# One GpSimd instruction of 1024 columns, with one signal, in place of two of 512 for the low part of a weight tile

## The chip, the cores and the metric

The kernel runs on one core of one Trainium2 chip. The metric is the device time of one execution in microseconds (us). The kernel before takes 1486.04 us, the median of three runs (1485.71 to 1487.81).

## The reference

The reference is one inference step of a two-layer decoder trunk with four parallel token mixers. There are 512 prompt tokens and 8 sample tokens, so every activation has 520 columns once it is transposed. What matters here, per layer:

```python
mod = silu(c) @ ada_w + ada_b                       # shift, scale, gate
h = rms_norm(x, norm_g) * (1.0 + scale) + shift
proj = einsum('btd,de->bte', h, w_in)               # (520, 1024) @ (1024, 7560)
oA, oB, oC, oD = rwkv7(...), retention(...), rglru(...), gated_delta(...)   # each 256 wide
up = einsum('btnw,nwd->btnd', stack(oA, oB, oC, oD), w_up)
merged = sum_n(sigmoid(gl) * up)                    # gl: the last 4 * 1024 columns of proj
x = x + gate * (merged @ w_out)
```

Two such layers are followed by an RMSNorm. All of it is in float32.

## The kernel before, in words

**Tiles and parts.** The products with `w_in`, `w_out` and `ada_w` are made in two parts: weights and activations are each split into a high part (a rounded copy) and a low part (the rest), and TensorE (PE) sums high by high, low by high and high by low. A weight tile is 1024 rows by 128 columns, in SBUF 128 partitions by 1024 columns. It comes by a transfer that SyncE issues (`load`, L559 for `ada_w`, L576 for `w_out` and `w_in`), then ScalarE (ACT) casts it to the high part (`split`, L1441), then GpSimd (POOL) subtracts the high part from it and leaves the low part in the place of the weights (L710). There are 94 tiles in layer 0 and 78 in layer 1: 30 `proj`, 32 `gate` and 8 `out` in each, and 24 or 8 `ada`, which make the next modulation rows. GpSimd does nothing else but clear some tiles at the start.

**Order of use on PE.** `product` (L838 and L846) takes a `proj`, `gate` or `out` tile in 12 parts: eight parts of four matmuls with the high part (k = 0 to 7), then four parts of four matmuls with the low part. It waits for GpSimd's first half ahead of low k = 0 and for the second half ahead of low k = 4. `ada` (L1373, L1376) has two matmuls with the high part and two with the low part, with a wait ahead of each of the latter. Tiles go through three ring slots, five in the last stage; a load into a slot is issued when PE has finished the tile that was there, and ACT splits a tile only when PE has finished with an earlier high part. Every engine works through its list in the order in which the code has it, and all signals are semaphores counted.

**The merge tail.** After the mixers a layer has 14 last lift products, `up(18)` to `up(31)` (L888), with an `ada` tile behind most of them (layer 1: behind the last eight), and then the eight `out` products. `up(n)` waits until VectorE (DVE) has emptied the PSUM pair that `up(n-2)` used. For each `up` DVE runs L1911 (reads PSUM and one SBUF tile) and L1912 (the same), and from `up(25)` on also `m_lo` (L1894): it subtracts the high part of a finished merged row from the row, both in SBUF. ACT makes that high part in `m_hi` (L1799), behind the split of the next weight tile in its list. The text numbers the eight `m_lo` from 0 to 7. `out(0)` is the first product that needs them, one for each k. In SyncE's list a `load` stands behind `bring_back` (L600), which waits for DVE's merged rows, and behind the end of the tile on PE whose slot it refills.

**Elsewhere.** In the trees (triangular solves) of the mixers DVE merges blocks with predicated copies (L797, L798), which PE waits for (L774), with parts of `proj` and `gate` tiles put between them. Ahead of the retention mixer DVE applies the rotation (L2277, L2279, L2281, L2289).

Of the kernel before, what the change touches and what calls it, by code (L numbers as in the profile page):

```python
# [19 lines left out]
KT = D_MODEL // P  # L20
# [57 lines left out]
def build_program(nc, a, o, order):  # L78
# [5 lines left out]
    mult, add, sub = ALU.mult, ALU.add, ALU.subtract  # L84
    ctx = ExitStack()
    tracks = {}
    with ctx:
# [193 lines left out]
        def ring_slot(kind, n, L):  # L281

            r = L.place[kind, n]
            return L.slot[r], (L.w[L.slot[r]], 16 * L.loads[r])

        def first_load(sp, n, L, layer):

            s, (arrived, _) = ring_slot("proj", n, L)
            col, _, _ = PROJ[n]
            sp.dma_start(RS[s], a["w_in"][layer, :, col:col + P].rearrange("(k p) c -> p k c", p=P)).then_inc(arrived, 16)  # L290
# [40 lines left out]
        @block.sync  # L331
        def _(sp):
            sp.dma_start(RC[0:8, 2:4, 0:512], a["c_sample"].rearrange("p (a c) -> p a c", a=2)).then_inc(s_c, 16)
            sp.dma_start(RC[8:9, 2:4, 0:512], a["c_prompt"].rearrange("p (a c) -> p a c", a=2)).then_inc(s_c, 16)
            sp.dma_start(cst[:, 0:384], a["consts"][:, 0:384]).then_inc(s_const, 16)
            sp.dma_start(RC[0:8, 0:2, 0:512], a["x_sample"][:, 0, :].rearrange("p (a c) -> p a c", a=2)).then_inc(s_c, 16)
            sp.dma_start(prow[0:PARAM_N, :], a["param_rows"][0]).then_inc(s_par, 16)
            lo = CONST_COLS["kdec"][0]
            sp.dma_start(cst[:, lo:CONST_N], a["consts"][:, lo:CONST_N]).then_inc(s_const, 16)
            for t in range(4):  # L340
                sp.dma_start(hT[:, 2 * t:2 * t + 2, 0:512], a["x_prompt"][0, t * P:(t + 1) * P, :].rearrange("p (a c) -> p a c", a=2)).then_inc(s_x, 16)
            for e in range(8):
                sp.dma_start(pairs[e], a["ada_w"][0, 512 * (e % 2):512 * (e % 2) + 512, 512 * (e // 2):512 * (e // 2) + 512]
                             .rearrange("(k p) c -> p k c", p=P)).then_inc(s_ada0[e], 16)
            for n in range(RING):
                first_load(sp, n, LAYERS[0], 0)
            sp.wait_ge(*dve0.at("x", KT - 1))
            for half in (slice(0, 4), slice(4, 8)):
                sp.dma_start(scrX[:, half, :], xT[:, half, :]).then_inc(LAYERS[0].xout, 16)
            sp.dma_start(cst[:, 384:lo], a["consts"][:, 384:lo]).then_inc(s_const2, 16)  # L350
            sp.dma_start(wv(10, 14 * P), a["tree_masks"]).then_inc(s_const2, 16)
# [112 lines left out]
        for layer, L in enumerate(LAYERS):  # L464
# [8 lines left out]
            aw, pw = TR["act_w"], TR["pool_w"]  # L473
            pm, am, dm = TR["pe_m"], TR["act_m"], TR["dve_m"]
            ps_, as_, ds = TR["pe_s"], TR["act_s"], TR["dve_s"]
            def ada_bank(b):

                return 2 if b in (1, 3) else 1
# [5 lines left out]
            def tile_part(ap, x):  # L484

                if x[0] == "proj" and PROJ[x[1]][1] == "ba":
                    return ap[:, :, 0:64].rearrange("p k (e c) -> p k e c", e=2)[:, :, :, 0:HEADS]
                return ap
# [215 lines left out]
            @block.gpsimd  # L704
            def _(pool):
                for q, (kind, n) in enumerate(SPLIT):
                    s, _ = ring_slot(kind, n, L)
                    pool.wait_ge(*aw.at("hi", q))
                    for k in (slice(0, KT // 2), slice(KT // 2, KT)):
                        nc.gpsimd.tensor_tensor(tile_part(RL[s][:, k], (kind, n)), tile_part(RS[s][:, k], (kind, n)), tile_part(HS[L.hslot[q]][:, k], (kind, n)), sub).then_inc(*pw.step("lo"))  # L710

# [104 lines left out]
            def _(pe):  # L818
# [5 lines left out]
                def product(out, x, kind, n, hi, lo, m=P, wait=None, parts=range(PARTS)):  # L824


                    s, _ = ring_slot(kind, n, L)
                    q = SPLACE[kind, n]
                    cols = lambda ap, h: ap[:, h * HALF:(h + 1) * HALF]
                    for p in parts:  # L830
                        if p == 0:
                            pe.wait_ge(*aw.at("hi", q))
                        if p < KT:
                            if wait:
                                pe.wait_ge(*wait(p))
                            for part in (hi, lo):
                                for h in x:
                                    nc.tensor.matmul(out(h), HS[L.hslot[q]][:, p, 0:m], cols(part(p), h), start=(p == 0 and part is hi), stop=False)  # L838
                            continue
                        if p == KT:  # L840
                            pe.wait_ge(*pw.at("lo", 2 * q))
                        elif p == KT + 2:
                            pe.wait_ge(*pw.at("lo", 2 * q + 1))
                        for k in (2 * (p - KT), 2 * (p - KT) + 1):
                            for h in x:
                                last = nc.tensor.matmul(out(h), RL[s][:, k, 0:m], cols(hi(k), h), start=False, stop=(k == KT - 1))  # L846
                    return last if parts[-1] == PARTS - 1 else None
# [516 lines left out]
                def ada(n):  # L1364

                    q, b, kp = SPLACE["ada", n], n // 4, n % 4
                    s, _ = ring_slot("ada", n, L)
                    out = psB[0:18, ada_bank(b), :]
                    pe.wait_ge(*aw.at("hi", q))
                    if b >= 2 and kp == 0:  # L1370
                        pe.wait_ge(*act_f.at("modrow", b - 1 if b == 5 else b - 2))
                    for k in range(2):
                        nc.tensor.matmul(out, chl[:, 2 * kp + k, :], wide(HS[L.hslot[q]])[:, k, :], start=(kp == 0 and k == 0), stop=False)  # L1373
                    for k in range(2):
                        pe.wait_ge(*pw.at("lo", 2 * q + k))
                        last = nc.tensor.matmul(out, chl[:, 2 * kp + k, :], wide(RL[s])[:, k, :], start=False, stop=(kp == 3 and k == 1))  # L1376
                    last.then_inc(*pe_f.step("ada"))
                    if kp == 1 and b:
                        mods(b - 1)
# [1048 lines left out]
    'pe_p0': 'proj proj proj proj proj proj proj proj proj proj proj proj proj proj proj proj proj proj proj proj proj proj proj proj proj proj proj proj proj proj'.split(),  # L2428
    'act_p0': 'proj proj proj proj proj proj proj proj proj proj proj proj proj proj proj proj proj proj proj proj proj proj proj proj proj proj proj proj proj proj'.split(),
    'act_w0': 'hi hi hi hi hi hi hi hi hi hi hi hi hi hi hi hi hi hi hi hi hi hi hi hi hi hi hi hi hi hi hi hi hi hi hi hi hi hi hi hi hi hi hi hi hi hi hi hi hi hi hi hi hi hi hi hi hi hi hi hi hi hi hi hi hi hi hi hi hi hi hi hi hi hi hi hi hi hi hi hi hi hi hi hi hi hi hi hi hi hi hi hi hi hi'.split(),  # L2430
    'pool_w0': 'lo lo lo lo lo lo lo lo lo lo lo lo lo lo lo lo lo lo lo lo lo lo lo lo lo lo lo lo lo lo lo lo lo lo lo lo lo lo lo lo lo lo lo lo lo lo lo lo lo lo lo lo lo lo lo lo lo lo lo lo lo lo lo lo lo lo lo lo lo lo lo lo lo lo lo lo lo lo lo lo lo lo lo lo lo lo lo lo lo lo lo lo lo lo lo lo lo lo lo lo lo lo lo lo lo lo lo lo lo lo lo lo lo lo lo lo lo lo lo lo lo lo lo lo lo lo lo lo lo lo lo lo lo lo lo lo lo lo lo lo lo lo lo lo lo lo lo lo lo lo lo lo lo lo lo lo lo lo lo lo lo lo lo lo lo lo lo lo lo lo lo lo lo lo lo lo lo lo lo lo lo lo lo lo lo lo lo lo'.split(),
    'pe_n0': 'mean var var var'.split(),
    'act_n0': 'sq ln rn tz sq ln rn tz tz sq ln rn tz'.split(),
    'dve_n0': 'cen normed gains bonus siluz gated normed siluz gated siluz gated normed siluz gated'.split(),
# [21 lines left out]
    'pe_p1': 'proj proj proj proj proj proj proj proj proj proj proj proj proj proj proj proj proj proj proj proj proj proj proj proj proj proj proj proj proj proj'.split(),  # L2456
    'act_p1': 'proj proj proj proj proj proj proj proj proj proj proj proj proj proj proj proj proj proj proj proj proj proj proj proj proj proj proj proj proj proj'.split(),
    'act_w1': 'hi hi hi hi hi hi hi hi hi hi hi hi hi hi hi hi hi hi hi hi hi hi hi hi hi hi hi hi hi hi hi hi hi hi hi hi hi hi hi hi hi hi hi hi hi hi hi hi hi hi hi hi hi hi hi hi hi hi hi hi hi hi hi hi hi hi hi hi hi hi hi hi hi hi hi hi hi hi'.split(),
    'pool_w1': 'lo lo lo lo lo lo lo lo lo lo lo lo lo lo lo lo lo lo lo lo lo lo lo lo lo lo lo lo lo lo lo lo lo lo lo lo lo lo lo lo lo lo lo lo lo lo lo lo lo lo lo lo lo lo lo lo lo lo lo lo lo lo lo lo lo lo lo lo lo lo lo lo lo lo lo lo lo lo lo lo lo lo lo lo lo lo lo lo lo lo lo lo lo lo lo lo lo lo lo lo lo lo lo lo lo lo lo lo lo lo lo lo lo lo lo lo lo lo lo lo lo lo lo lo lo lo lo lo lo lo lo lo lo lo lo lo lo lo lo lo lo lo lo lo lo lo lo lo lo lo lo lo lo lo lo lo'.split(),
    'pe_n1': 'mean var var var'.split(),  # L2460
    'act_n1': 'sq ln rn tz sq ln rn tz tz sq ln rn tz'.split(),
    'dve_n1': 'cen normed gains bonus siluz gated normed siluz gated siluz gated normed siluz gated'.split(),
# [108 lines left out]
```

## Time and profile before

| | |
|---|---|
| median of three runs | 1486.04 us |
| the profiled execution | 1487.9 us, of it 1486.1 us from the first to the last instruction |
| PE busy | 1406.4 us, 95% |
| DVE, ACT, POOL busy | 652.1, 517.0, 466.5 us |
| granted TensorE clock, mean | 0.981 of full speed |

Busy times say how much an engine did, not whether anything waited for it. The chain that ended last, and who waited for whom, say what set the time. In rows of a timeline the first number is the start in us from the first instruction, the second the time to the end of the last of the "xN" instructions that the row merges; in brackets stands the idle time before the first and what ended it.

### The profile page before, as it was taken

What the parts mean: (1) busy time and instruction counts of PE and PEld (TensorE: products, weight loads), DVE (VectorE), ACT (ScalarE), POOL (GpSimd) and SP (SyncE); (2) the same over time, 40 slices, a digit from 0 to 9 for tenths busy, and PEclk for the clock granted to TensorE, in tenths of its full rate; (3) what the DMA queues carried; (4) which work ended last, traced back from release to release, by engine and by line L of the source; (5) the groups of instructions that cost most, each with busy time, mean ns of one, the idle gap of its engine ahead of it and who ended that gap; (6) DMA issues with size and microseconds to landing.
All of it is one profiled execution on the core that took longest, in us unless ns stands there. A gap on an engine that the chain in (4) does not pass through costs nothing.

```text
span 1486.1 us, 33569 instructions
## 1 busy us (share of the span) xinstructions
PE 1406.4 (95%) x14880; PEld 1275.5 (86%) x14880; DVE 652.1 (44%) x1157; ACT 517.0 (35%) x780; POOL 466.5 (31%) x350
## 2 busy tenths in 40 slices
PE   6799999999999999998979999999999999998896
PEld 4699999989889998876879998999898998987695
DVE  5757423317234335746133951231444341655712
ACT  5534422225422245144443352222443123523312
POOL 0244422224212223147833452222322222312720
PEclk9899999999999999999999999999999999999998
DMA  9533231215321263376743323112263126346721
GB/s 318 196 86 97 68 91 45 59 45 118 102 81 45 68 128 98 117 221 215 228 143 86 98 74 84 45 45 73 65 153 85 45 59 103 99 143 176 222 86 58
DMA packets 275908, 162.18 MB, mean 109 GB/s; under 512 B 86102, under 2 KB 244922, under 8 KB 275252
## 3 DMA queue, kind: packets, MB, share of 16 engines
q1 hardware_dynamic: 274100, 159.06, 39.2%
q8 instruction: 117, 1.92, 0.5%
q10 hardware_dynamic: 1664, 0.98, 0.3%
q14 instruction: 27, 0.22, 0.0%
HBM read 135.25 MB, written 24.89 MB: 108 GB/s over the span
## 4 chain that ended last, share of the span: by engine, by line
PE 84%; DVE 6%; ACT 4%; DMA 2%; issue 2%; ACTq 1%; SPq 0%; POOL 0%; DVEq 0%
PE psA L838 35%; PE psA L846 18%; PE psA L888 6%; PE psB L774 3%; PE psB L784 3%; PE psB L783 3%; PE psB L719 2%; PE psB L962 1%; DMA RB<-in_ada_w 1%; PE psB L972 1%; PE psB L1376 1%; PE psB L1373 1%; PE psB L1404 1%; ACT w_hi L1441 1%; DMA RB<-in_w_out 1%
## 5 line engine op out<-in xcount | busy, mean ns | idle before, releaser
L710 POOL TENSOR_TENSOR w_lo<-ring,w_hi 128x512 fp32r<-128x512 f32 x274 | 372.4, 1381 | 901.9 <-ACT w_hi L1441 843.9
L838 PE MATMUL psA<-h_hi,w_hi 128*128 128x260 f32 x1984 | 427.4, 297 | 23.2 <-DVE h_lo L1856 13.1
L838 PE MATMUL psA<-h_lo,w_hi 128*128 128x260 f32 x1984 | 403.5, 285 | 0.0
L838 PEld LDWEIGHTS psA<-h_hi,w_hi 128*128 128x128 f32 x1984 | 309.2, 191 | 39.8 <-issue 19.6
L838 PEld LDWEIGHTS psA<-h_lo,w_hi 128*128 128x128 f32 x1984 | 310.1, 191 | 0.2
L846 PE MATMUL psA<-h_hi,w_lo 128*128 128x260 f32 x1984 | 274.5, 286 | 0.0
L846 PEld LDWEIGHTS psA<-h_hi,w_lo 128*128 128x128 f32 x1984 | 249.6, 187 | 5.3 <-issue 1.0
L1441 ACT CAST w_hi<-ring 128x1024 fp32r<-128x1024 f32 x133 | 137.2, 1033 | 14.1 <-PE psA L846 4.1
L789 ACT COPY ws<-psB 128x128 f32<-128x128 f32 x80 | 21.4, 268 | 243.9 <-PE psB L774 243.9
L797 DVE COPY_PREDICATED tg<-tmask,psB 128x128 f32<-128x128 uint8 x40 | 14.3, 357 | 127.2 <-PE psB L784 77.4
L1471 ACT ACTIVATE tg<-psA 128x520 f32<-128x520 f32 x48 | 28.9, 601 | 87.9 <-PE psA L846 87.7
L797 DVE COPY_PREDICATED ws<-tmask,psB 128x128 f32<-128x128 uint8 x40 | 14.3, 356 | 83.4 <-PE psB L784 46.8
L2354 DVE SCALAR_TENSOR_TENSOR xT<-psA,modT,xT 128x260 f32<-128x260 f32 x16 | 7.8, 488 | 90.1 <-PE psA L846 90.0
L710 POOL TENSOR_TENSOR w_lo<-ring,ra_lo 128x512 fp32r<-128x512 f32 x28 | 37.6, 1363 | 22.9 <-ACT ra_lo L1441 22.9
L710 POOL TENSOR_TENSOR rb_lo<-RB,ra_lo 128x512 fp32r<-128x512 f32 x20 | 25.5, 1300 | 42.1 <-ACT ra_lo L1441 42.1
L784 PE MATMUL psB<-tg,ws 64*64 64x32 f32 x640 | 37.4, 220 | 0.0
L784 PE MATMUL psB<-ws 64*64 64x32 f32 x640 | 37.4, 220 | 0.0
L888 PE MATMUL psA<-RB,upw 128*128 128x260 f32 x128 | 32.3, 396 | 3.6 <-DVE RA L1912 3.2
L1456 ACT COPY RA<-psA 128x520 f32<-128x520 f32 x18 | 10.7, 593 | 66.8 <-PE psA L846 61.6
L888 PEld LDWEIGHTS psA<-RB,upw 128*128 128x128 f32 x128 | 24.2, 194 | 10.4 <-DVE RA L1912 4.2
L784 PEld LDWEIGHTS psB<-tg,ws 64*64 64x64 f32 x640 | 32.1, 135 | 1.1
L784 PEld LDWEIGHTS psB<-ws 64*64 64x64 f32 x640 | 32.1, 135 | 1.1
(476 smaller groups left out, 2332.1 us busy)
## 6 DMA issues: line engine op xcount, KB each, us to landing
ring<-in_w_in SPq DMA_DIRECT2D x122, 512.0 KB, 4.2
scr_tanh<-tg SPq DMA_DIRECT2D x48, 260.0 KB, 4.5
ring<-in_ada_w SPq DMA_DIRECT2D x18, 512.0 KB, 5.2
upw<-in_w_up SPq DMA_DIRECT2D x64, 128.0 KB, 3.6
RA<-scr_tanh SPq DMA_DIRECT2D x30, 260.0 KB, 3.6
RB<-in_ada_w SPq DMA_DIRECT2D x14, 512.0 KB, 5.0
ws<-scr_tanh SPq DMA_DIRECT2D x24, 260.0 KB, 3.9
ring<-in_w_out SPq DMA_DIRECT2D x9, 512.0 KB, 4.9
```

The lines of the kernel that those rows point to most:

```text
L710: nc.gpsimd.tensor_tensor(tile_part(RL[s][:, k], (kind, n)), tile_part(RS[s][:, k], (kind, n)), tile_part(HS[L.hslot[q]][:, k], (kind, n)) ...
L719: last = nc.tensor.matmul(psB[:, k, 0:HALF], bones, s4[:, k, :], start=True, stop=True)
L774: last = nc.tensor.matmul(meet(psB[sd(g), 2, q * CH:(q + 1) * CH], lv, 0), At[sd(g), q, :], meet(T4[sd(g), q, :], lv, 0), start=True, stop ...
L783: nc.tensor.matmul(meet(psB[sd(g), 2, q * CH:(q + 1) * CH], lv, 0), V4[sd(g), q, :], meet(Y4[sd(g), q, :], lv, 0), start=True, stop=True)
L784: last = nc.tensor.matmul(meet(psB[sd(g), 2, 256 + q * CH:256 + (q + 1) * CH], lv, 1), Y4[sd(g), q, :], meet(V4[sd(g), q, :], lv, 1), star ...
L789: nc.scalar.copy(meet(q64(Y), lv, 0), meet(q64(psB[:, 2, 0:256]), lv, 0)).then_inc(*ta.step("y"))
L797: nc.vector.copy_predicated(meet(q64(T), lv, 0), bc(meet(tmask[:, lv, :], lv, 0), 1, 4), meet(q64(psB[:, 2, 0:256]), lv, 0))
L838: nc.tensor.matmul(out(h), HS[L.hslot[q]][:, p, 0:m], cols(part(p), h), start=(p == 0 and part is hi), stop=False)
L846: last = nc.tensor.matmul(out(h), RL[s][:, k, 0:m], cols(hi(k), h), start=False, stop=(k == KT - 1))
L888: last = nc.tensor.matmul(out(hf), upw[:, idx % UP_RING, i, :], outs[MERGE[idx][0]][:, i, hf * HALF:(hf + 1) * HALF], start=(i == 0), stop ...
L1441: nc.scalar.copy(tile_part(HS[L.hslot[q]], SPLIT[q]), tile_part(RS[s], SPLIT[q])).then_inc(*aw.step("hi"))
L1471: A(half(th_tile(idx)), psA[:, b:b + 2, 0:HALF], ACT.Tanh, scale=0.5).then_inc(*am.step("th"))
```

## The change

GpSimd makes the low part of a tile in one instruction over all eight k instead of two over four each, and signals once. PE waits for that one signal ahead of the first matmul with the low part, in `product` and in `ada`. The lists of signals are cut to half (`pool_w0` from 188 to 94 names, `pool_w1` from 156 to 78).

```diff
                     pool.wait_ge(*aw.at("hi", q))
-                    for k in (slice(0, KT // 2), slice(KT // 2, KT)):
-                        nc.gpsimd.tensor_tensor(tile_part(RL[s][:, k], (kind, n)), tile_part(RS[s][:, k], (kind, n)), tile_part(HS[L.hslot[q]][:, k], (kind, n)), sub).then_inc(*pw.step("lo"))
+                    nc.gpsimd.tensor_tensor(tile_part(RL[s], (kind, n)), tile_part(RS[s], (kind, n)), tile_part(HS[L.hslot[q]], (kind, n)), sub).then_inc(*pw.step("lo"))
...
                         if p == KT:
-                            pe.wait_ge(*pw.at("lo", 2 * q))
-                        elif p == KT + 2:
-                            pe.wait_ge(*pw.at("lo", 2 * q + 1))
+                            pe.wait_ge(*pw.at("lo", q))
...
+                    pe.wait_ge(*pw.at("lo", q))
                     for k in range(2):
-                        pe.wait_ge(*pw.at("lo", 2 * q + k))
                         last = nc.tensor.matmul(out, chl[:, 2 * kp + k, :], wide(RL[s])[:, k, :], start=False, stop=(kp == 3 and k == 1))
```

## Rows read from the trace of the kernel before

**Rows 1.** The page: busy time by engine, and the chain that ended last

```profile
PE 1406.4 (95%) x14880; PEld 1275.5 (86%) x14880; DVE 652.1 (44%) x1157; ACT 517.0 (35%) x780; POOL 466.5 (31%) x350
...
PE 84%; DVE 6%; ACT 4%; DMA 2%; issue 2%; ACTq 1%; SPq 0%; POOL 0%; DVEq 0%
```

**Rows 2.** PE's waits: waiting tile and line, releaser: total us, times, longest

```profile
PE psA L838 <- DVE merged_lo L1894: 4.9, 4, 1.5
...
PE psA L888 <- DVE RA L1912: 4.0, 4, 2.0
...
PE psB L1376 <- POOL rb_lo L710: 1.5, 2, 0.8
```

**Rows 3.** Line L710: count, duration ns min/median/max, first and last start

```profile
L710 POOL TENSOR_TENSOR w_lo<-ring,ra_lo x28: 1264/1286/1757, 662.6 to 1426.0; 128x512 fp32r<-128x512 f32 x28
```

**Rows 4.** GpSimd's groups by shape: count, busy us, mean ns of one, idle before

```profile
L710 POOL TENSOR_TENSOR w_lo<-ring,w_hi 128x32 fp32r<-128x32 f32 x4 | 0.9, 252 | 0.0
```

**Rows 5.** Line L846: all idle time of its engine before it, us and times

```profile
  issue: 1.0, 6
```

**Rows 6.** Timelines, layer 0, `out` stage: an `ada` tile on GpSimd and on PE

```profile
718.55 2.53 POOL L710 TENSOR_TENSOR rb_lo<-RB,ra_lo 128x512 fp32r<-128x512 f32 x2 [0.94 <-ACT ra_lo L1441]
...
721.95 0.62 PE L1376 MATMUL psB<-rb_lo,c_parts 128*18 128x512 f32 x2
```

**Rows 7.** Timelines, layer 0, the first `ada` tile on GpSimd and on PE

```profile
652.69 3.75 POOL L710 TENSOR_TENSOR rb_lo<-RB,ra_lo 128x512 fp32r<-128x512 f32 x3 [16.27 <-ACT ra_lo L1441]
...
655.26 0.40 PE L1376 MATMUL psB<-rb_lo,c_parts 128*18 128x512 f32 x1 [0.83 <-POOL rb_lo L710]
```

**Rows 8.** Line L1894 (all 16 `m_lo`): mean ns after the busy time

```profile
L1894 DVE TENSOR_TENSOR merged_lo<-mg,merged_hi 128x520 fp32r<-128x520 f32 x10 | 14.5, 1468 | 6.1 <-ACT merged_hi L1799 6.1
...
L1894 DVE TENSOR_TENSOR ra_lo<-RA,merged_hi 128x520 fp32r<-128x520 f32 x6 | 9.3, 1552 | 8.5 <-ACT merged_hi L1799 8.5
...
L2158 DVE TENSOR_TENSOR RD<-RD,ws 128x512 f32<-128x512 f32 x4 | 2.6, 684 | 0.0
```

**Rows 9.** DVE's timeline in the merge tail of layer 0

```profile
679.26 1.35 DVE L1894 TENSOR_TENSOR ra_lo<-RA,merged_hi 128x520 fp32r<-128x520 f32 x1 [4.47 <-ACT merged_hi L1799]
...
689.36 1.34 DVE L1894 TENSOR_TENSOR merged_lo<-mg,merged_hi 128x520 fp32r<-128x520 f32 x1 [1.55 <-ACT merged_hi L1799]
...
698.59 3.06 DVE L1894 TENSOR_TENSOR merged_lo<-mg,merged_hi 128x520 fp32r<-128x520 f32 x2 [0.23 <-ACT merged_hi L1799]
```

**Rows 10.** GpSimd's timeline in the same tail

```profile
678.78 2.96 POOL L710 TENSOR_TENSOR w_lo<-ring,ra_lo 128x512 fp32r<-128x512 f32 x2 [0.46 <-ACT ra_lo L1441]
...
688.87 2.98 POOL L710 TENSOR_TENSOR w_lo<-ring,ra_lo 128x512 fp32r<-128x512 f32 x2 [1.27 <-ACT ra_lo L1441]
...
698.13 2.96 POOL L710 TENSOR_TENSOR rb_lo<-RB,w_hi 128x512 fp32r<-128x512 f32 x2
```

**Rows 11.** PE's timeline in the same tail

```profile
682.02 2.02 PE L888 MATMUL psA<-RB,upw 128*128 128x260 f32 x8 [1.25 <-DVE RA L1912]
...
701.70 0.51 PE L838 MATMUL psA<-merged_hi,ra_lo 128*128 128x260 f32 x2 [0.94 <-DVE merged_lo L1894]
```

**Rows 12.** SyncE's timeline in the same tail: two issues of `w_out` tiles

```profile
683.10 0.40 SPq L576 DMA_DIRECT2D ring<-in_w_out  x1
...
691.75 0.37 SPq L576 DMA_DIRECT2D RB<-in_w_out  x1
```

**Rows 13.** Windows: length, busy PE, PEld, DVE, ACT, POOL, granted clock, DMA

```profile
675.00:692.00 17.00, 15.47 (x70) 10.30 (x70) 11.05 (x12) 8.52 (x12) 14.31 (x10) 1.00 0.90 291
1385.00:1400.00 15.00, 13.05 (x55) 8.55 (x53) 9.47 (x11) 6.77 (x9) 10.82 (x9) 0.89 0.81 254
1406.00:1423.00 17.00, 14.50 (x102) 13.84 (x103) 8.31 (x12) 3.93 (x6) 8.30 (x6) 0.90 0.33 104
```

**Rows 14.** Timelines of GpSimd, DVE and PE in the first tree of layer 0

```profile
190.73 2.57 POOL L710 TENSOR_TENSOR w_lo<-ring,w_hi 128x512 fp32r<-128x512 f32 x2 [9.99 <-ACT w_hi L1441]
...
191.08 1.23 DVE L798 COPY_PREDICATED tg<-tmask,ws 128x128 f32<-128x128 uint8 x1
...
193.16 0.54 PE L774 MATMUL psB<-tg,ws 64*64 64x32 f32 x12
```

**Rows 15.** DVE's timeline at the rotation in layer 0

```profile
572.52 2.33 DVE L2279 SCALAR_TENSOR_TENSOR RB<-RB,cst 128x520 f32<-128x520 f32 x2
```

More of the change, by code:

```diff
@@ L2430 @@
     'act_w0': 'hi hi hi hi hi hi hi hi hi hi hi hi hi hi hi hi hi hi hi hi hi hi hi hi hi hi hi hi hi hi hi hi hi hi hi hi hi hi hi hi hi hi hi hi hi hi hi hi hi hi hi hi hi hi hi hi hi hi hi hi hi hi hi hi hi hi hi hi hi hi hi hi hi hi hi hi hi hi hi hi hi hi hi hi hi hi hi hi hi hi hi hi hi hi'.split(),
-    'pool_w0': 'lo lo lo lo lo lo lo lo lo lo lo lo lo lo lo lo lo lo lo lo lo lo lo lo lo lo lo lo lo lo lo lo lo lo lo lo lo lo lo lo lo lo lo lo lo lo lo lo lo lo lo lo lo lo lo lo lo lo lo lo lo lo lo lo lo lo lo lo lo lo lo lo lo lo lo lo lo lo lo lo lo lo lo lo lo lo lo lo lo lo lo lo lo lo lo lo lo lo lo lo lo lo lo lo lo lo lo lo lo lo lo lo lo lo lo lo lo lo lo lo lo lo lo lo lo lo lo lo lo lo lo lo lo lo lo lo lo lo lo lo lo lo lo lo lo lo lo lo lo lo lo lo lo lo lo lo lo lo lo lo lo lo lo lo lo lo lo lo lo lo lo lo lo lo lo lo lo lo lo lo lo lo lo lo lo lo lo lo'.split(),
+    'pool_w0': 'lo lo lo lo lo lo lo lo lo lo lo lo lo lo lo lo lo lo lo lo lo lo lo lo lo lo lo lo lo lo lo lo lo lo lo lo lo lo lo lo lo lo lo lo lo lo lo lo lo lo lo lo lo lo lo lo lo lo lo lo lo lo lo lo lo lo lo lo lo lo lo lo lo lo lo lo lo lo lo lo lo lo lo lo lo lo lo lo lo lo lo lo lo lo'.split(),
     'pe_n0': 'mean var var var'.split(),
@@ L2458 @@
     'act_w1': 'hi hi hi hi hi hi hi hi hi hi hi hi hi hi hi hi hi hi hi hi hi hi hi hi hi hi hi hi hi hi hi hi hi hi hi hi hi hi hi hi hi hi hi hi hi hi hi hi hi hi hi hi hi hi hi hi hi hi hi hi hi hi hi hi hi hi hi hi hi hi hi hi hi hi hi hi hi hi'.split(),
-    'pool_w1': 'lo lo lo lo lo lo lo lo lo lo lo lo lo lo lo lo lo lo lo lo lo lo lo lo lo lo lo lo lo lo lo lo lo lo lo lo lo lo lo lo lo lo lo lo lo lo lo lo lo lo lo lo lo lo lo lo lo lo lo lo lo lo lo lo lo lo lo lo lo lo lo lo lo lo lo lo lo lo lo lo lo lo lo lo lo lo lo lo lo lo lo lo lo lo lo lo lo lo lo lo lo lo lo lo lo lo lo lo lo lo lo lo lo lo lo lo lo lo lo lo lo lo lo lo lo lo lo lo lo lo lo lo lo lo lo lo lo lo lo lo lo lo lo lo lo lo lo lo lo lo lo lo lo lo lo lo'.split(),
+    'pool_w1': 'lo lo lo lo lo lo lo lo lo lo lo lo lo lo lo lo lo lo lo lo lo lo lo lo lo lo lo lo lo lo lo lo lo lo lo lo lo lo lo lo lo lo lo lo lo lo lo lo lo lo lo lo lo lo lo lo lo lo lo lo lo lo lo lo lo lo lo lo lo lo lo lo lo lo lo lo lo lo'.split(),
     'pe_n1': 'mean var var var'.split(),
```

## The prediction

> **What bounds the kernel now.** I read the page first. PE is busy 95% of the span and is 84% of the chain that ended last; GpSimd is busy 31% and is 0% of that chain, DVE is 6% of it [rows 1]. So an instruction saved on GpSimd pays only where something waits for GpSimd. The list of PE's waits says where that is: PE waited for GpSimd twice in the whole span, 1.5 us together, against 4.9 and 4.0 us for DVE's L1894 and L1912 in the merge tails [rows 2]. The timelines then say who those DVE instructions wait for, and that turns out to be GpSimd after all: not its signal, but its running instruction. That is where I expect the change to show.
>
> **The instruction itself.** 172 pairs of 512 columns become 172 single ones (for the two `ba` tiles the pair is of 32 columns). Undisturbed, 512 columns take 1286 ns [rows 3] and 32 take 252 ns [rows 4]: (1286 − 252) / 480 = 2.15 ns a column. So 1024 columns take 1286 + 512 × 2.15 = 2390 ns, against 2.53 us for a pair, whose two parts overlap a little [rows 6]. The whole low part is there 0.14 us sooner, its first half 1.1 us later. On GpSimd this saves some 172 × 0.14 = 24 us, all of it off the chain.
>
> **PE's waits.** The wait that goes, ahead of low k = 4, costs nothing now: all idle time before L846 in the span is 1.0 us, all of it "issue" and none of it a wait [rows 5]. What replaces it is an earlier need for the whole tile. In order of tiles I compared PE's first use of each low part with the end of its pair. In all but one of the 172 the pair is done before PE asks for its first half, as the two waits in the list say [rows 2]. The least lead is that of an `ada` tile: done at 718.55 + 2.53 = 721.08, first matmul at 721.95 [rows 6]. Cost zero; the cover is PE's own work on the high part and on tiles ahead. The one exception is the first `ada` tile of layer 0. Its second half is done about 655.2 and its last matmul starts at 655.26 [rows 7]; now all is done at 652.69 + 2.39 = 655.08, but both matmuls come behind that, 0.22 us more than one (0.62 against 0.40) [rows 6, 7]. Cost: **+0.1 us**.
>
> **DVE behind a longer GpSimd instruction.** All 16 `m_lo` (L1894) take 1468 to 1552 ns on average, where a subtraction-like instruction of the same size with two SBUF inputs takes 684 ns [rows 8]. The timelines show why. GpSimd starts at 678.78, so its first half ends near 680.06; `m_lo` 0 starts at 679.26 and ends at 680.61, 0.55 us after that end. GpSimd's second half then ends only at 681.74, 1.13 us after `m_lo` [rows 9, 10]. The two take turns: each waits until the other's instruction is over. `m_lo` comes some 0.5 us after GpSimd's start, since ACT makes the high part of the weight tile just before that of the merged row. Behind an instruction of 2.39 us it waits 1.1 us longer.
>
> What the trace doesn't show is an instruction longer than 512 columns. If GpSimd let DVE in halfway through 1024 columns, the cost would be nil; if it holds to the end, it is 1.1 us for each `m_lo` met early. I take the second, since in the rows no `m_lo` got in before an end.
>
> The Trainium skill, "SBUF — State Buffer", section "Who interferes with whom", states the same as a rule against this change: a DVE instruction with two SBUF inputs contends with a GpSimd instruction that reads SBUF, and whoever is first has the shared ports for its whole instruction. By that rule the sum below stands; were it not so at 1024 columns, the time would be that of the second rival. No row here shows it beyond 512 columns.
>
> **The merge tail, step by step (layer 0).** `m_lo` 0 ends at 678.78 + 2.39 + 0.55 = 681.72 instead of 680.61. L1911 and L1912 follow it in DVE's list, so `up(28)`, which waits for them at 682.02 [rows 11], starts 1.1 us later. The rest of the tail inherits this along two paths. SyncE's issue at 683.10 stands behind those merged rows, so it goes to 684.2. GpSimd starts 5.77 us after the issue [rows 10, 12], at 689.97, and ends at 692.36; `m_lo` 3 then ends at 692.9 instead of 690.70, 2.2 us late, and `up(31)` with it. The issue at 691.75 waits for an `ada` tile that PE ends ahead of `up(31)`, so it is only 1.1 us late, 692.85. GpSimd starts on that tile 6.38 us later [rows 10, 12], at 699.23, and ends at 701.62. `m_lo` 6 ends at 702.2, and `m_lo` 7 right behind it at 702.75: no second half steps between them, as one does now. Today the pair ends at 698.59 + 3.06 = 701.65 [rows 9] and PE goes on at 701.70 [rows 11]. Cost **+1.1 us**, not 8 × 1.1: delays in between fall into waits for transfers and the last one falls away. Layer 1 has the same eight `m_lo` and the same pattern: **+1.1 us**.
>
> **The clock.** PE's gap at 682.02 grows from 1.25 [rows 11] to 2.35 us. In layer 1 the same gap is 2.0 us [rows 2], and the window around it was granted 0.89 of full speed, where that of layer 0 had 1.00 [rows 13]. 0.11 × 15 us = 1.7 us of full-speed work lost, a stretch at 1.2 instead of 2.4 GHz behind idle time. From zero (layer 0 stays at full speed) to 3.4 us (a further such stretch in layer 1 too), I take one more stretch, in layer 0, nearest to the layer 1 row: **+1.7 us**.
>
> **Two small places.** In the first tree L798 reads two SBUF tiles and waits for GpSimd's first half; behind a whole one it ends at 190.73 + 2.39 + 0.3 = 193.4, and PE wants it at 193.16 [rows 14]: **+0.3 us**; its like in layer 1 fits. At the rotation L2279 waits for the end of a pair (2.33 us for two that take about 0.7 each) [rows 15]; the pair's end comes 0.14 us sooner, in two layers: **−0.3 us**. DVE work that waits for GpSimd elsewhere has idle time behind it.
>
> **Sum.** 0.1 + 2.2 + 1.7 + 0.3 − 0.3 = 4.0 us. The profiled execution (1487.9 us, span 1486.1) becomes 1491.9. It lies 1.9 us above the median of the runs, which is no part of the change, so against the median of 1486.04 I forecast **1490.0 us**, 0.27% slower. A measurement of this kernel can tell about 0.2%, 3.0 us, from no change.
>
> **Rivals.**
> *No new slow stretch.* All as above but the clock: +2.3 us, 1488.3, within 0.2%. For it: layer 0 kept full speed over its gap of 1.25 us; against it: layer 1 did not over 2.0.
> *The cover holds.* GpSimd gives way inside its instruction, or the 1.1 us is lost in the waits for transfers that `m_lo` 0 and 3 already stand behind (4.47 and 1.55 us idle before them [rows 9]). Then 0.1 − 0.3, 1485.8.
> *Not slower: the last turn decides.* If the transfer at 691.75 came as early as now, GpSimd's last tile would run from 698.13 to 700.5 [rows 10], `m_lo` 6 end at 701.1 and `m_lo` 7, with no second half before it, at 701.65: no loss in the tails. PE would then idle less just before `out(0)`, where layer 1 now loses 0.10 × 17 = 1.7 us of clock [rows 13]. Without that stretch: 0.1 + 0.3 − 0.3 − 1.7 = −1.6, 1484.4. It decides where that issue no longer waits for a late `ada`; against it, PE works without a gap from the late `up(28)` to that tile.
> *The delays add up.* If each tail ends with the 2.2 us that `m_lo` 3 has, and both layers get a slow stretch more: 0.1 + 4.4 + 3.4 = +7.9, 1493.9.
>
> **How the numbers follow.** Chances: forecast 0.42, no new stretch 0.25, cover 0.17, last turn 0.06, adding up 0.10. The predicted time is the forecast's. The range goes from 1485.6, just below the case in which the cover holds, to 1493.0, most of the way to the case in which delays add; it leaves out the last turn and part of that case. Slower by over 0.2%: 0.42 + 0.10, less a little for a forecast that comes out smaller, 0.50. Within 0.2%: 0.25 + 0.17 and that little, 0.44. Faster by over 0.2%: 0.06.
>
> **What would show it.** Right: L710 once a tile near 2.4 us; L1894 near 2.4 us where it meets GpSimd early; PE's wait at `up(28)` near 2.3 us in layer 0; the last `m_lo` no longer waiting; the window of layer 0's tail below 1.00. Wrong: L1894 as long as before (GpSimd gives way), PE's waits at L838 and L888 in the tails unchanged, or new waits for L710 at L846 (a lead that I missed).

## The result, and the profile after

The changed kernel took 1489.46 us (median of 12 runs, 1485.69 to 1493.96) against 1485.40 us for the kernel before in the same set (12 runs, 1481.18 to 1488.07): ratio 1.0030, 95% interval 1.0017 to 1.0043. A second set, below, gave 1.0003. All measurements together put the change at 1.5 us (± 0.7), 0.1%, slower; how that is taken from runs that scatter by several us is told with the experiments. The profiled execution has a span of 1487.3 us at a mean granted clock of 0.980.

The page of the changed kernel, busy time by engine and the chain that ended last; the lines that answer to [rows 1]:

```profile
PE 1407.6 (95%) x14880; PEld 1277.9 (86%) x14880; DVE 681.4 (46%) x1157; ACT 517.2 (35%) x780; POOL 423.0 (28%) x178
...
PE 83%; DVE 7%; ACT 4%; DMA 2%; issue 2%; ACTq 1%; SPq 0%; POOL 0%; DVEq 0%
```

GpSimd works 43.5 us less, and DVE "works" 29.3 us more with the same 1157 instructions. That is time in which a DVE instruction has started and waits. Only 5.2 us of it are in the 16 `m_lo` (17.6 + 11.4 against 14.5 + 9.3 us, the busy times below and in [rows 8]). GpSimd's groups by shape (count, busy us, mean ns of one, idle before):

```profile
L709 POOL TENSOR_TENSOR w_lo<-ring,w_hi 128x1024 fp32r<-128x1024 f32 x135 | 338.0, 2505 | 935.5 <-ACT w_hi L1438 876.9 <-ACT w_hi L296 58.5
L709 POOL TENSOR_TENSOR w_lo<-ring,ra_lo 128x1024 fp32r<-128x1024 f32 x14 | 33.2, 2373 | 28.1 <-ACT ra_lo L1438 28.1
...
L709 POOL TENSOR_TENSOR rb_lo<-RB,ra_lo 128x1024 fp32r<-128x1024 f32 x10 | 23.6, 2369 | 43.2 <-ACT ra_lo L1438 43.2
```

The two `m_lo` groups, which answer to [rows 8]:

```profile
L1891 DVE TENSOR_TENSOR merged_lo<-mg,merged_hi 128x520 fp32r<-128x520 f32 x10 | 17.6, 1778 | 3.6 <-ACT merged_hi L1796 3.6
...
L1891 DVE TENSOR_TENSOR ra_lo<-RA,merged_hi 128x520 fp32r<-128x520 f32 x6 | 11.4, 1903 | 6.4 <-ACT merged_hi L1796 6.4
```

PE's waits (us in total, times, longest), to hold against [rows 2]:

```profile
PE psA L837 <- DVE merged_lo L1891: 4.0, 2, 2.3
PE psA L885 <- DVE RA L1909: 3.8, 4, 2.0
...
PE psB L1373 <- POOL rb_lo L709: 1.8, 1, 1.8
...
PE psA L885 <- DVE mg L1909: 1.4, 1, 1.4
PE psA L837 <- DVE mg L1909: 1.3, 1, 1.3
...
PE psB L773 <- DVE tg L797: 0.4, 2, 0.3
```

Still only the first `ada` tile is waited for at GpSimd itself. What has changed stands at DVE: the wait in the trees (L773) is new, the one at `up(31)` has grown from 0.4 to 1.4 us, and where `out(0)` waited twice for a merged row, 0.9 us together, it waits once, 1.3 us. The merge tail of layer 0 shows how they arise; GpSimd, DVE and PE in the changed kernel's timeline, as in [rows 9 to 11]:

```profile
676.33 2.36 POOL L709 TENSOR_TENSOR w_lo<-ring,ra_lo 128x1024 fp32r<-128x1024 f32 x1 [0.47 <-ACT ra_lo L1438]
...
687.34 2.37 POOL L709 TENSOR_TENSOR w_lo<-ring,ra_lo 128x1024 fp32r<-128x1024 f32 x1 [2.80 <-ACT ra_lo L1438]
...
696.28 2.37 POOL L709 TENSOR_TENSOR rb_lo<-RB,w_hi 128x1024 fp32r<-128x1024 f32 x1 [0.62 <-ACT w_hi L1438]
```

```profile
676.81 2.44 DVE L1891 TENSOR_TENSOR ra_lo<-RA,merged_hi 128x520 fp32r<-128x520 f32 x1 [3.48 <-ACT merged_hi L1796]
...
687.82 2.44 DVE L1891 TENSOR_TENSOR merged_lo<-mg,merged_hi 128x520 fp32r<-128x520 f32 x1 [1.37 <-ACT merged_hi L1796]
...
697.49 2.33 DVE L1891 TENSOR_TENSOR merged_lo<-mg,merged_hi 128x520 fp32r<-128x520 f32 x2
```

```profile
680.66 2.02 PE L885 MATMUL psA<-RB,upw 128*128 128x260 f32 x8 [1.33 <-DVE RA L1909]
...
691.66 2.02 PE L885 MATMUL psA<-RB,upw 128*128 128x260 f32 x8 [1.42 <-DVE mg L1909]
...
699.27 0.51 PE L837 MATMUL psA<-merged_hi,ra_lo 128*128 128x260 f32 x2 [1.66 <-DVE merged_lo L1891]
```

`m_lo` 0 starts at 676.81, in the middle of a GpSimd instruction that ends at 676.33 + 2.36 = 678.69, and ends at 679.25, 0.56 us after it: 2.44 us, as forecast. `m_lo` 3 does the same (2.44). The last two take 2.33 us together, against 3.06 in [rows 9]: the last one finds GpSimd idle. PE's three gaps are 1.33, 1.42 and 1.66 us, 4.4 in all. Before, there were 1.25 at `up(28)` and 0.94 at the end [rows 11], with 0.38 at `up(31)` and 0.31 and 1.53 us ahead of and in `out(0)` between: 4.4 in all as well. In this pair of profiles the tail of layer 0 has moved its waits and idles no longer than before; that of layer 1 idles 5.6 us for 4.9.

### The profile page after: what moved, and what is told of

Read it like the earlier page. It is cut to its first block, busy times and chain, and to the rows that moved or that the text cites. A ratio compares the mean times of both kernels' runs of the same rounds, so it can differ in the third digit from the quotient of the medians.

```text
span 1487.3 us, 33397 instructions
## 1 busy us (share of the span) xinstructions
PE 1407.6 (95%) x14880; PEld 1277.9 (86%) x14880; DVE 681.4 (46%) x1157; ACT 517.2 (35%) x780; POOL 423.0 (28%) x178
## 4 chain that ended last, share of the span: by engine, by line
PE 83%; DVE 7%; ACT 4%; DMA 2%; issue 2%; ACTq 1%; SPq 0%; POOL 0%; DVEq 0%
PE psA L837 35%; PE psA L843 18%; PE psA L885 5%; PE psB L773 3%; PE psB L783 3%; PE psB L782 3%; PE psB L718 2%; PE psB L959 1%; PE psB L969 1%; PE psB L1401 1%; DMA RB<-in_ada_w 1%; PE psB L1373 1%; PE psB L1370 1%; PE psB L765 1%; ACT w_hi L1438 1%
## 5 line engine op out<-in xcount | busy, mean ns | idle before, releaser
L709 POOL TENSOR_TENSOR w_lo<-ring,w_hi 128x1024 fp32r<-128x1024 f32 (+1 forms) x137 | 338.5, 2473 | 935.5 <-ACT w_hi L1438 876.9
L1438 ACT CAST w_hi<-ring 128x1024 fp32r<-128x1024 f32 x133 | 137.2, 1033 | 14.4 <-PE psA L843 4.2
L709 POOL TENSOR_TENSOR w_lo<-ring,ra_lo 128x1024 fp32r<-128x1024 f32 x14 | 33.2, 2373 | 28.1 <-ACT ra_lo L1438 28.1
L709 POOL TENSOR_TENSOR rb_lo<-RB,ra_lo 128x1024 fp32r<-128x1024 f32 x10 | 23.6, 2369 | 43.2 <-ACT ra_lo L1438 43.2
L885 PEld LDWEIGHTS psA<-RB,upw 128*128 128x128 f32 x128 | 24.1, 194 | 11.6 <-DVE RA L1909 4.3
```

What stands on the lines that cost most here:

```text
L709: nc.gpsimd.tensor_tensor(tile_part(RL[s], (kind, n)), tile_part(RS[s], (kind, n)), tile_part(HS[L.hslot[q]], (kind, n)), sub).then_inc(*p ...
L885: last = nc.tensor.matmul(out(hf), upw[:, idx % UP_RING, i, :], outs[MERGE[idx][0]][:, i, hf * HALF:(hf + 1) * HALF], start=(i == 0), stop ...
L1438: nc.scalar.copy(tile_part(HS[L.hslot[q]], SPLIT[q]), tile_part(RS[s], SPLIT[q])).then_inc(*aw.step("hi"))
```

## The experiments

**How times are compared.** Runs of one kernel scatter by several us, and most of that goes with the mean granted clock of each run. Fitted within kernels, over all sets, a run is 1.18 us shorter for each 0.001 of clock. The column "at 0.982" moves each kernel's mean to that clock, with twice its standard error. It leaves out whatever part of a difference comes from a lower clock, and it was first used after the four experiments of the second set. "Idle in tails" comes from each one's profile: the sum of PE's gaps over 0.1 us between the same instructions, from the last lift products to `out(1)` (in the kernel before 660 to 706 and 1376 to 1423 us), both layers added. After the set of the result three more were run, each with its own runs of the kernel before (27 to 35; those of the first set have no clock on record). Most kernels have 12 runs, before_mhi_first 6, before_mhi_again 10, quarters_again 4.

| kernel | median us | ratio to before, 95% | at 0.982 | idle in tails |
|---|---|---|---|---|
| before (first profile; all three sets) | 1485.93, 1487.54, 1487.20 | 1 | 1486.4, 1486.8, 1486.7 (± 0.6) | 9.3 |
| before_again | 1487.81 | 1.0012 [0.9994, 1.0030] | 1486.7 ± 1.3 | 9.2 |
| the changed kernel | 1489.46 | 1.0030 [1.0017, 1.0043] | 1488.3 ± 0.8 | 10.0 |
| after_again | 1486.00 | 1.0003 [0.9983, 1.0023] | 1487.9 ± 0.8 | 11.6 |
| one_wait | 1486.06 | 0.9995 [0.9975, 1.0015] | 1486.0 ± 1.1 | 8.1 |
| tail_halves | 1484.84 | 0.9993 [0.9971, 1.0015] | 1485.3 ± 1.1 | 11.4 |
| tail_whole | 1488.13 | 1.0007 [0.9990, 1.0024] | 1487.6 ± 0.8 | 11.8 |
| before_mhi_first | 1478.20 | 0.9941 [0.9921, 0.9962] | 1479.7 ± 0.9 | 4.3 |
| before_mhi_again | 1476.88 | 0.9941 [0.9921, 0.9961] | 1479.5 ± 1.2 | 4.6 |
| tail_halves_mhi | 1480.03 | 0.9967 [0.9941, 0.9993] | 1480.3 ± 1.2 | 4.7 |
| after_mhi_first | 1483.73 | 0.9987 [0.9971, 1.0003] | 1482.0 ± 0.9 | 7.2 |
| quarters | 1492.75 | 1.0030 [1.0007, 1.0053] | 1488.2 ± 2.0 | 14.4 |
| quarters_again | 1494.59 | 1.0070 [1.0043, 1.0097] | 1490.5 ± 0.9 | 13.4 |
| quarters_mhi_first | 1485.10 | 1.0005 [0.9986, 1.0023] | 1484.3 ± 1.1 | 8.2 |

**The later signal alone.** The two instructions stay, but PE waits for the second ahead of its first matmul with the low part.

```diff
                         if p == KT:
-                            pe.wait_ge(*pw.at("lo", 2 * q))
-                        elif p == KT + 2:
                             pe.wait_ge(*pw.at("lo", 2 * q + 1))
...
+                    pe.wait_ge(*pw.at("lo", 2 * q + 1))
                     for k in range(2):
-                        pe.wait_ge(*pw.at("lo", 2 * q + k))
```

> Two GpSimd instructions of 512 columns a tile as before; only PE's signal is changed: it waits once, for the second half, ahead of the first matmul with the low part. Theory A (DVE waits for the running GpSimd instruction in the merge tails): the instruction is as short as before, so the time is that of the kernel before, ratio 0.999 to 1.001, m_lo (L1894) 1.47 and 1.55 us on average. Theory B (the later signal costs): as slow as the change, ratio near 1.003, with new PE waits for L710.

Measured: 1486.06 us, ratio 0.9995, no difference. The first `ada` tile is waited for once and longer, as in the changed kernel, and nothing else. The cost of the change does not come from PE's waits for GpSimd.

**Where the length of the instruction matters.** In one kernel `ada` and `out` tiles, the ones that `m_lo` meets, are cut in halves and the others whole; the other kernel (`kind not in`) has it the other way round.

```diff
+            CUTS = [2 if kind in ("ada", "out") else 1 for kind, _ in SPLIT]
+            LO = [sum(CUTS[:r]) for r in range(len(CUTS))]
...
-                    for k in (slice(0, KT // 2), slice(KT // 2, KT)):
+                    w = KT // CUTS[q]
+                    for k in [slice(w * c, w * c + w) for c in range(CUTS[q])]:
...
```

PE waits ahead of the first low part of a tile that is whole, and ahead of each half of one that is cut.

> One instruction of 1024 columns for the proj and gate tiles, two of 512 with two signals for the ada and out tiles of the merge tail. Theory A: the loss is in the tails, so it goes: ratio 0.999 to 1.001, the tree's +0.3 us left, m_lo 1.47 and 1.55 us. Theory C (the longer instruction holds up DVE in the mixers, where 124 of the 172 tiles are): ratio near 1.003.

> The other way round: two of 512 for proj and gate, one of 1024 for the 48 ada and out tiles. Theory A: nearly all of the change's loss, ratio 1.002 to 1.003, m_lo near 2 us on average with those that meet GpSimd early at 2.4. Theory C: 0.999 to 1.001.

> The changed kernel once more, for a second profile. Both theories: ratio 1.002 to 1.004. If the tail's loss depends on how long the transfers of the ada tiles take, PE's shift against the kernel before differs at up(28) from that of the first profile (0 us there), and the half-speed stretches fall elsewhere.

Measured: both ratios, and that of the changed kernel beside them, hold 1 in their intervals; by ratios alone this set tells nothing, and the two that were expected at 1.002 and more came out at 1.0007 and 1.0003. At equal clock the order is the one that the mechanism asks for: 1485.3 with halves in the tails, 1487.6 with whole ones there, 1487.9 with whole ones everywhere. In tail_whole both groups of `m_lo` are as long as in the changed kernel (columns as above):

```profile
L1898 DVE TENSOR_TENSOR merged_lo<-mg,merged_hi 128x520 fp32r<-128x520 f32 x10 | 17.5, 1764 | 5.3 <-ACT merged_hi L1803 5.3
...
L1898 DVE TENSOR_TENSOR ra_lo<-RA,merged_hi 128x520 fp32r<-128x520 f32 x6 | 10.9, 1822 | 7.3 <-ACT merged_hi L1803 7.3
```

In tail_halves they are as in the kernel before:

```profile
L1898 DVE TENSOR_TENSOR merged_lo<-mg,merged_hi 128x520 fp32r<-128x520 f32 x10 | 15.0, 1518 | 7.9 <-ACT merged_hi L1803 7.8
...
L1898 DVE TENSOR_TENSOR ra_lo<-RA,merged_hi 128x520 fp32r<-128x520 f32 x6 | 9.3, 1556 | 8.0 <-ACT merged_hi L1803 8.0
```

So `m_lo` follows the tiles of the tail alone. The idle time in the tails does so less clearly: 9.5 us on average over the four profiles with halves there, 11.2 over the three with whole ones, but tail_halves has 11.4, so one profile could not have told. One of PE's gaps tells them apart in every profile: the one at `up(31)` in layer 0 is 0.38, 0.35, 0.24 and 0.49 us in the four profiles with halves (before, before_again, one_wait, tail_halves), and 1.42, 1.43 and 2.11 us in the three with whole instructions (after, after_again, tail_whole). The one at `up(28)` in layer 1 leans the same way, 1.95, 1.50, 1.70 and 1.48 us against 1.96, 2.63 and 2.92. PE in tail_halves and in tail_whole:

```profile
688.67 2.02 PE L891 MATMUL psA<-RB,upw 128*128 128x260 f32 x8 [0.49 <-DVE mg L1916]
```

```profile
691.57 2.02 PE L891 MATMUL psA<-RB,upw 128*128 128x260 f32 x8 [2.11 <-DVE mg L1916]
```

**The order in ACT's list.** The two tails depend on when ACT makes the high part of a merged row. Here it comes ahead of the split of the next tile.

```diff
                 for i in range(14):
+                    if i >= 7:
+                        m_hi(i - 7)
                     if 18 + i in L.up_piece:
                         mod_rows(L.up_piece[18 + i])
-                    if i >= 7:
-                        m_hi(i - 7)
```

> The changed kernel, but ACT makes the high part of a merged row ahead of the split of the next weight tile, not behind it. Theory A (m_lo is late because it meets GpSimd's running instruction): m_lo 0 and most others start while GpSimd is idle or nearly done, so their mean falls from some 1.8 us towards 0.7 to 1.2 us; PE's gaps in the two tails, 4.4 and 5.6 us in the changed kernel's profile, shrink by 1 to 3 us each; 2 to 5 us faster than the changed kernel, so 1482 to 1485 us against a kernel before of 1486. Rival T (the tails wait for transfers, m_lo fills only waits): m_lo gets shorter, but PE's gaps and the time stay within 1 us of the changed kernel's.

> The kernel before with the same exchange in ACT's list. Theory A: m_lo shorter here too, less to gain since a GpSimd instruction holds it up for 1.29 us and not 2.4: 1 to 4 us faster than the kernel before. If m_lo no longer meets GpSimd, this and the kernel with whole instructions and the same exchange come out within 1 us of each other at the same granted clock: then the change's cost was this meeting alone. Rival T: both as without the exchange, this one about 1 us faster than the one with whole instructions.

> The kernel before with the exchange in ACT's list, once more, beside the others of this set. If the first measurement was no accident of few executions: 5 to 8 us below the kernel before, ratio 0.994 to 0.997, and PE's gaps ahead of up(28), up(31) and out(0) shorter in both tails. If it was one: within 3 us of the kernel before.

Measured: this is the version that beats both kernels. With halves it takes 0.9941 of the time of the kernel before, 1478.20 and 1476.88 us in two sets, and 7 us less at equal clock; with whole instructions it is 0.9987, and 6 us below the changed kernel at equal clock. With halves that is more than the 1 to 4 us expected. The reason that theory A gave is wrong, though. `m_lo` does not get out of GpSimd's way; the groups of after_mhi_first and then of before_mhi_first:

```profile
L1891 DVE TENSOR_TENSOR merged_lo<-mg,merged_hi 128x520 fp32r<-128x520 f32 x10 | 20.3, 2042 | 1.5 <-ACT merged_hi L1796 1.5
...
L1891 DVE TENSOR_TENSOR ra_lo<-RA,merged_hi 128x520 fp32r<-128x520 f32 x6 | 10.5, 1745 | 1.7 <-ACT merged_hi L1796 1.7
```

```profile
L1894 DVE TENSOR_TENSOR merged_lo<-mg,merged_hi 128x520 fp32r<-128x520 f32 x10 | 14.9, 1487 | 4.1 <-ACT merged_hi L1799 4.0
...
L1894 DVE TENSOR_TENSOR ra_lo<-RA,merged_hi 128x520 fp32r<-128x520 f32 x6 | 8.2, 1367 | 2.0 <-ACT merged_hi L1799 2.0
```

What goes is DVE's idle time before them, 8.5 us ahead of the six in [rows 8] and 2.0 here. DVE's and ACT's timelines in the kernel before show what it was; the first is DVE's last instruction on the merged row that `m_lo` 0 needs:

```profile
671.42 0.70 DVE L1912 TENSOR_TENSOR RA<-psA,RA 128x520 f32<-128x520 f32 x1
```

```profile
677.66 1.05 ACT L1441 CAST ra_lo<-ring 128x1024 fp32r<-128x1024 f32 x1 [1.92 <-DMA ring<-in_ada_w]
678.61 0.62 ACT L1799 CAST merged_hi<-RA 128x520 fp32r<-128x520 f32 x1
```

The row was ready at 672.12, but ACT waited for a transfer to split a tile that came first in its list. With the exchange the high part for `m_lo` 0 stands one split earlier, in before_mhi_first behind the one at 671.97:

```profile
671.97 1.04 ACT L1441 CAST ra_lo<-ring 128x1024 fp32r<-128x1024 f32 x1 [3.38 <-DMA ring<-in_ada_w]
672.92 0.62 ACT L1799 CAST merged_hi<-RA 128x520 fp32r<-128x520 f32 x1
...
675.93 0.62 ACT L1799 CAST merged_hi<-RA 128x520 fp32r<-128x520 f32 x1
```

`up(28)` and `up(31)` then wait for nothing in either layer, and the tails' idle time falls to 4.3 and 4.6 us with halves. With whole instructions 7.2 us stay, nearly all of it ahead of and in `out(0)`; PE's waits in before_mhi_first and in after_mhi_first:

```profile
PE psA L838 <- DVE merged_lo L1894: 3.8, 3, 1.9
```

```profile
PE psA L837 <- DVE merged_lo L1891: 7.0, 4, 2.1
```

That is the change's price with nothing else in front of it: 7.2 − 4.5 = 2.7 us of idle time, and 1482.0 − 1479.6 = 2.4 us at equal clock. The medians lie further apart, 1483.73 against 1478.20 and 1476.88 us, since the runs also differ in clock: a mean of 0.9802 with whole instructions and of 0.9837 with halves (± 0.0016 on the difference). In the profile with whole instructions the clock granted around `out(0)`, where its longer waits are, was 0.79 in both layers (688 to 704 and 1399 to 1415 us), in the three profiles with the exchange and halves in the tails between 0.89 and 1.00. Whether this loss of clock belongs to the change was not tested; if it does, the price is nearer to 6 us than to 2.4. Some 2 of the exchange's 7 us are not in the tails' idle time of these profiles; where they went was not settled.

**Halves for the tail only, with the exchange.** The edits of tail_halves and of the exchange together.

> Whole instructions of 1024 columns for proj and gate tiles, halves of 512 for ada and out tiles (the ones that m_lo meets), and in ACT's list the high part of a merged row ahead of the split. Theory A (all of the change's cost is m_lo behind a running instruction in the tails; elsewhere whole ones cost nothing): within 1 us of the kernel with halves everywhere and the same exchange at the same granted clock, so about 1479 us against 1486.5 for the kernel before, and some 2 us below whole instructions with the exchange (1482). Rival E (whole instructions cost elsewhere too: tree, rotation, first ada): at 1482 like those.

Measured: 1480.3 ± 1.2 at equal clock, 0.7 from the kernel with halves everywhere and 1.7 below whole ones; idle in tails 4.7 us. Theory A fits better than rival E, though the errors are nearly as large as the differences: whole instructions outside the tails cost nothing that shows, nor do they bring anything.

**The kernel before against itself.**

> The kernel before, unchanged, against itself: shows what a comparison of this length can tell from nothing, and what of the shifts between two profiles is the place of the half-speed stretches. Expected ratio 1.000 with an interval of 0.002 to each side that holds 1; m_lo's durations 1.34 to 1.77 us again, each ending 0.55 us after a GpSimd instruction; half-speed stretches in other places than in the first profile.

Measured: ratio 1.0012 [0.9994, 1.0030]. A difference of 0.1 to 0.2% in one set is therefore nothing to build on, and the 0.3% of the first set needed the equal-clock comparison beside it. In layer 0 PE had no gap at `up(28)` here and one of 0.35 us at `up(31)`, where the first profile of the same kernel has 1.25 and 0.38: the gap at `up(28)` of layer 0 comes and goes without any change.

**Four instructions of 256 columns.** If shorter is better, quarters should be best.

```diff
-                    for k in (slice(0, KT // 2), slice(KT // 2, KT)):
+                    for k in [slice(2 * c, 2 * c + 2) for c in range(4)]:
...
-                        if p == KT:
-                            pe.wait_ge(*pw.at("lo", 2 * q))
-                        elif p == KT + 2:
-                            pe.wait_ge(*pw.at("lo", 2 * q + 1))
+                        pe.wait_ge(*pw.at("lo", 4 * q + p - KT))
...
```

> The change turned round: four instructions of 256 columns with a signal each, and PE waits for each ahead of the two parts of four matmuls that need it. By the rows at 32 and 512 columns one takes 252 + 224 x 2.15 = 734 ns, so a tile takes 2.9 us and not 2.53 or 2.39. Theory A: m_lo waits at most 0.7 us for GpSimd, its mean is 1.0 to 1.4 us; PE's gap at up(28) is 0.5 us shorter than with halves; last m_lo up to 0.7 us later, a step in again; time 0 to 1.5 us below the kernel before. Rival N (the number of instructions and signals costs): 172 x 0.4 us more on GpSimd, new waits of PE for the low part, and DVE's turns with GpSimd elsewhere; 1 to 3 us above the kernel before.

> Quarters and the exchange in ACT's list together. Theory A: at or a little below the better of the two, 1481 to 1485 us. If the exchange alone takes m_lo out of GpSimd's way, the size of GpSimd's instruction no longer matters, and this, the one with halves and the one with whole instructions lie within 1 us of one another at the same granted clock. Rival N: 1 to 3 us above the one with halves and the exchange.

> Four instructions of 256 columns, once more. Theory S (DVE is not given a turn at every end of a GpSimd instruction; where it misses one, a queue of back-to-back instructions keeps it out until GpSimd runs dry): one or more DVE instructions with two SBUF inputs, m_lo 0 of layer 0 first of all, last over 3 us and span many GpSimd ends, and executions with such a stall lie some 6 to 9 us above those without. Rival (the 9.8 us of the first profile were one accident): all m_lo below 1.4 us and times near the kernel before.

Measured: slower than the kernel before, 1.0030 and 1.0070, and the reason is neither of the two first named. Most `m_lo` are as short as theory A wanted, but one is not; DVE and then GpSimd in quarters:

```profile
678.02 9.77 DVE L1891 TENSOR_TENSOR ra_lo<-RA,merged_hi 128x520 fp32r<-128x520 f32 x1 [3.07 <-ACT merged_hi L1796]
689.06 0.69 DVE L1891 TENSOR_TENSOR ra_lo<-RA,merged_hi 128x520 fp32r<-128x520 f32 x1
```

```profile
676.23 5.56 POOL L710 TENSOR_TENSOR w_lo<-ring,ra_lo 128x256 fp32r<-128x256 f32 x8
681.75 5.48 POOL L710 TENSOR_TENSOR rb_lo<-RB,w_hi 128x256 fp32r<-128x256 f32 x8
```

A DVE instruction of 0.69 us lasted 9.77 us. Fourteen GpSimd instructions ended while it waited, and it ended 0.56 us after the last of them, at 681.75 + 5.48 = 687.23, when GpSimd had nothing more. PE paid for it:

```profile
689.19 3.40 PE L885 MATMUL psA<-RB,upw 128*128 128x260 f32 x7 [8.24 <-DVE RA L1909]
```

The same `m_lo` was held up in all three profiles with quarters (9.77, 9.62 and 9.65 us), and so was an addition of 128x8 at 733 to 740 us (3.86, 7.02 and 10.45 us where it takes 0.17); DVE in quarters_again:

```profile
678.26 9.65 DVE L1891 TENSOR_TENSOR ra_lo<-RA,merged_hi 128x520 fp32r<-128x520 f32 x1 [3.19 <-ACT merged_hi L1796]
...
739.84 10.45 DVE L2354 TENSOR_TENSOR xT<-xT,der 128x8 f32<-128x8 f32 x1
...
751.31 0.17 DVE L2354 TENSOR_TENSOR xT<-xT,der 128x8 f32<-128x8 f32 x1
```

Theory S is borne out in the profiles, but for the 3.86 us: there the addition came in between two tiles of a row that went on. The clock is lower besides: 0.83 was granted from 675 to 705 us in quarters and in quarters_again, against 1.00 and 0.89 in the two profiles of the kernel before, and the runs' mean clock is 0.979 against 0.982, so the column at 0.982 may show only a part of the price. That executions without such a stall are the short ones among the times of quarters (1482.92 to 1497.45) fits, but was not seen, as each kernel has one profile. In those with 512 or 1024 columns no DVE instruction that was held up waited past more than one end. Why DVE gets its turn at the first end in nearly all cases with quarters, and not in these, stays open.

With the exchange quarters come to 1484.3 us at equal clock, 4.7 above halves and 2.3 above whole instructions with the same exchange. The expectation that the three sizes would lie within 1 us is missed for the reason given above, that the exchange doesn't take `m_lo` out of GpSimd's way: `m_lo` 0 was held up for 9.62 us here too, and `up(28)` waited 5.53 us.

## Why the prediction was right, and where its sum was not

The forecast was 1490.0 us, 0.27% slower, and the first set gave 1489.46, 0.30% slower. The sign and the mechanism were right. The sum of 4.0 us was not: it was some 2.5 us too large. That the forecast lies 0.5 us from the first set is luck; over all runs the change costs 1.5 us.

- **The instruction**: 2390 ns forecast; 2369 to 2373 where GpSimd is undisturbed. Right. GpSimd saves 43.5 us and not 24, off the chain as forecast.
- **PE's waits**: zero but for the first `ada` tile, and so it is; one_wait shows it without the longer instruction.
- **DVE to the end of the running instruction**: right at 1024 columns too. `m_lo` took up to 2.45 us, each ending about 0.55 us after GpSimd's end. The Trainium skill, "SBUF — State Buffer", section "Who interferes with whom", has the holder keep the shared ports for its whole instruction, and these rows agree with it. But "1.1 us for each met early" went to six of the 16 `m_lo` only; on average they grew by 0.31 and 0.35 us, since a late one meets its GpSimd instruction nearer to the end.
- **The merge tail, step by step**: this step was mis-sized. The gap at `up(28)` was forecast at 2.35 us and was 1.33: the transfer that the whole tail hangs on took 5.08 us from issue to split and not 6.06 as in the profile before, which is about the difference. The forecast stood on one profile of a gap that varies by itself, from 0 to 1.31 us over the four with halves. At `up(31)` the lateness came as forecast (a gap of 1.42 for 0.38), and at the end the last `m_lo` no longer waited, as forecast, so `out(0)` waited 1.66 us and not 2.78 (0.31, 1.53 and 0.94). The two tails idle 10.0 us for 9.3, and over all profiles 11.2 for 9.5: +1.7, where the sum had +2.2.
- **The clock**: the term of +1.7 us failed. The window of layer 0's tail stayed at full speed. The windows of the changed kernel (PE busy, granted clock, DMA share, GB/s), to hold against [rows 13]:

```profile
675.00:692.00 17.00, 14.25 (x66) 1.00 0.81 257
692.00:705.00 13.00, 11.34 (x65) 0.87 0.28 81
1385.00:1400.00 15.00, 13.04 (x52) 0.89 0.84 262
1406.00:1423.00 17.00, 13.35 (x91) 0.90 0.37 117
```

  This profile has a stretch at 1.2 GHz in layer 0 after all (0.50 granted from 701 to 704.3 us, behind the wait of 1.66 us), in the 13 us behind the window named, but such stretches fall elsewhere in each profile. The mean clock of the runs was 0.9812 and 0.9827 in two sets, that of the kernel before between 0.9808 and 0.9823. No loss of clock through the change is shown between these two kernels (with the exchange the clocks do differ, as told above). The first set's 0.3% holds a share of chance: at equal clock the cost is 1488.1 − 1486.6 = 1.5 us.
- **The tree**: +0.3 forecast. DVE's copy waits for the whole instruction, and PE for the copy, twice in the span (0.4 us):

```profile
191.00 2.37 POOL L709 TENSOR_TENSOR w_lo<-ring,w_hi 128x1024 fp32r<-128x1024 f32 x1 [10.09 <-ACT w_hi L1438]
191.41 2.27 DVE L797 COPY_PREDICATED tg<-tmask,ws 128x128 f32<-128x128 uint8 x1
...
193.82 0.39 PE L773 MATMUL psB<-tg,ws 64*64 64x32 f32 x7 [0.27 <-DVE tg L797]
```

- **The rotation**: PE's wait behind it fell from 0.38 to 0.24 us in both layers, −0.3 in all, as forecast. These two waits are part of the 4.0 us at L888 that the prediction put down to the merge tails alone; 3.2 us of it are there.

Of the rivals, "no new slow stretch" (+2.3 us) is nearest to what all runs together say. "The cover holds" falls with `m_lo` at 2.44 us, the longer waits at `up(31)` and the 2.4 us between the two kernels with the exchange. "Not slower" had the last turn right: in layer 0 of this pair of profiles `out(0)` gains the 1.1 us that `up(31)` loses. Its sum is wrong over all runs: the tail idles 4.3 us with halves and 5.2 with whole instructions in layer 0, 5.3 and 6.0 in layer 1, and the slow stretch that was to go from layer 1 stayed (0.90 in its window before and after).

## What to carry to other kernels

An instruction on an engine that nobody waits for can still be on the path, as the time for which another engine's instruction cannot run: look for DVE instructions with two SBUF inputs that end a fixed time after GpSimd's end, and count what the longest GpSimd instruction in that stretch would add. Shorter is not simply better: here 512 columns beat both 1024 and 256. Ahead of tuning either, look at what an in-order list puts in front of the late step: moving one short cast ahead of a split that waits for its transfer was worth over four times what the change cost at equal clock.

## What the runs showed of the hardware that was not expected

- DVE was kept out by a row of 14 or 15 GpSimd instructions of 256 columns, for 9.65 and 10.45 us, each of which began after DVE's own had started to wait, but for the first. The Trainium skill, "SBUF — State Buffer", section "Who interferes with whom", says that issue order decides who blocks. By that alone DVE should have come in at the first end, and these rows differ from it.
- The scatter of the runs is mostly granted clock: 1.18 us for each 0.001, with means between 0.974 and 0.988 for single runs. After that is taken out, 0.9 to 2.2 us stay for most kernels (standard deviation), and 3.5 us for quarters.
- The transfer that a tail hangs on took 5.08 and 6.06 us from its issue to the split, in two profiles of nearly the same kernel, as much of a difference as the change makes to `m_lo`.
